# Split products in two column halves, and two PSUM banks that take turns at every inner tile

## The chip, the cores and the metric

The kernel runs on one core of one Trainium2 chip. The metric is the device time of one execution in microseconds (us), the median of several runs of the same program.

## The reference, cut to what matters

The reference is two transformer-like blocks over 512 tokens of width 1024, in float32. The first has a modulated norm, one wide input projection, a gated convolution branch, a four-head mLSTM and a feed-forward of width 2816. The second has two layers: sparse latent attention and windowed attention, each with a small cross-attention to a memory and a feed-forward with a three-tap convolution. What the change touches is the dense products, all of this kind:

```
proj = jnp.einsum("bsd,de->bse", h, w_in[l]) + b_in[l]
gt, up = jnp.split(jnp.einsum("bsd,df->bsf", h, w_ffn_up[l]), 2, axis=-1)
x = x + g2 * jnp.einsum("bsf,fd->bsd", jax.nn.silu(gt) * up, w_ffn_down[l])
```

The feed-forward products occur three times, once for each block or layer.

## The kernel before

Activations lie transposed: 128 channels on the partitions, 512 tokens in the free dimension, one such tile for every 128 channels. A product therefore has a 128x128 weight tile as the stationary operand of TensorE and a 128x512 activation tile as the moving one, and it fills one PSUM bank (512 float32 values per partition).

To be exact enough at the speed of the fp32r type, each operand is split in a high and a low part (`h_hi`, `h_lo`; for weights the two parts of `w_split`). Each inner tile `c` is then three fp32r matmuls into the same bank: weights high with activations high, weights high with activations low, weights low with activations high. The program gives one instruction for each; the trace shows a weight load (PEld) and a matmul (PE) for it. Plain float32 matmuls, used for small things such as rotations and means, leave two pairs of records each.

The work is a fixed list of jobs (`STAGES`, with names such as `glu`, `ffn0_up0`, `ffn0_down0`). An ordinary job is a weight block of 8 inner tiles and 2 output tiles: 48 matmuls, 24 into each of the two banks `2p` and `2p+1`, where `p` is the parity of the job. The two parities are double buffers of weights and of banks. A feed-forward down job has one output tile and 12 or 10 inner tiles. SyncE loads the weights, ScalarE writes their high part, GpSimd subtracts to get the low part, and VectorE and ScalarE take the banks over. TensorE's order is written out by hand:

- `split_job` (L901) issues nearly all the jobs. Where `waits` is given, in the first job of a stage whose activations come tile by tile, its order is inner tile outside and output tile inside, so the two banks already take turns at every inner tile. Without `waits` it does all inner tiles of the first bank and then those of the second. `product_done[p]` is raised once, after the job's last matmul. `between` is a list of small pieces of other work, of which one is taken after each tile with an odd index `m * kc + c`.
- `first_part` and `second_part` (L1040, L1059) issue the first two `glu` jobs, `tile_product` (L1137) the `o` and `merge_mlstm` tiles, `heads_part` (L1358) output jobs that fill in attention, and L1445, L1471, L1485 and L1533 the jobs `a_qmem`, `a_uk`, `a_uv` and `b_qmem`.
- The jobs `v` (L1111) and `b_v` (L1520) are not touched. In them the roles are turned: an activation tile of 128x128 is stationary, and a weight tile of 128x256 is the moving operand, in the same three fp32r matmuls. Each has a weight load of its own, also where two in a row have the same stationary tile.
- `rotations` (L1288) are float32 matmuls on 512 columns that come through `between`, above all in `a_keys`, `a_kv`, `b_v` and `b_qmem`; VectorE takes their banks over.

Of the kernel before, what the change touches and what calls it, by code (L numbers as in the profile page):

```python
# [31 lines left out]
P = 128  # L32
T = 512
TB = T // P
D = 1024
DT = D // P
# [181 lines left out]
def build(nc, io):  # L218
    ctx = ExitStack()
    with ctx:  # L220
# [624 lines left out]
        def _(pe):  # L845
# [36 lines left out]
            def late_mean(norm):  # L882
# [4 lines left out]
                    nc.tensor.matmul(banks[6][:], con("mean_d"), square[:, 1, :], start=True, stop=True)  # L887
                nc.tensor.matmul(banks[4][:], con("mean_d"), rstd[:], start=True, stop=True).then_inc(S["late_mean"], 1)

            def split_job(p, kc, width, rhs, waits, tiles=2, split=None, between=(), late=None):  # L890


                between = list(between)
                w = [(split or w_split)[p][:, part, 0:kc * width].rearrange("p (c n) -> p c n", n=width) for part in range(2)]

                order = [(m, c) for c in range(kc) for m in range(tiles)] if waits else [(m, c) for m in range(tiles) for c in range(kc)]
                for m, c in order:
                    if waits and m == 0:
                        pe.wait_ge(S[waits[0]], waits[1] + c + 1)
                    for wp, hp in ((0, 0), (0, 1), (1, 0)):  # L900
                        last = nc.tensor.matmul(banks[2 * p + m][:], w[wp][:, c, m * P:(m + 1) * P], rhs(c, hp),  # L901
                                                start=(c == 0 and wp + hp == 0), stop=(c == kc - 1 and wp == 1))
                    if between and (m * kc + c) % 2 == 1:
                        between.pop(0)()
                    if late and (m, c) == (1, 5):
                        late_mean(late)
                assert not between
                last.then_inc(product_done[p], 1)
# [121 lines left out]
            def first_part(c, m):  # L1030

                if (c, m) == (0, 0):
                    pe.wait_ge(S["half_lower"], 1)
                    pe.wait_ge(bank_free[p], use + 1)
                if (c, m) == (DT // 2, 0):
                    pe.wait_ge(lo_ready[p], SPLITS_BEFORE[FIRST["glu"]] + 1)
                if m == 0:
                    pe.wait_ge(S["norm_ready"], c + 1)
                for wp, hp in ((0, 0), (0, 1), (1, 0)):
                    last = nc.tensor.matmul(banks[2 * p + m][:], w[wp][:, c, m * P:(m + 1) * P], h_parts(c, hp),  # L1040
                                            start=(c == 0 and wp + hp == 0), stop=(c == DT - 1 and wp == 1))
                if (c, m) == (DT - 1, 1):
                    last.then_inc(product_done[p], 1)

# [3 lines left out]
            def second_part(c):  # L1048

                if c == 0:  # L1050
                    pe.wait_ge(bank_free[p2], use2 + 1)
                    pe.wait_ge(S["half_lower"], 2)
                if c == DT // 2:
                    pe.wait_ge(lo_ready[p2], SPLITS_BEFORE[FIRST["glu"] + 1] + 1)
                for m in (1, 0):
                    if (c, m) == (0, 0):
                        pe.wait_ge(S["norm_scaled"], DT)
                    for wp, hp in ((0, 0), (0, 1), (1, 0)):
                        last = nc.tensor.matmul(banks[2 * p2 + m][:], w2[wp][:, c, m * P:(m + 1) * P], h_parts(c, hp),  # L1059
                                                start=(c == 0 and wp + hp == 0), stop=(c == DT - 1 and wp == 1))  # L1060
                if c == DT - 1:
                    last.then_inc(product_done[p2], 1)

# [62 lines left out]
            def tile_product(k, between=None):  # L1126

                name, j, m = ("o", "merge_mlstm")[k // 8], k % 8 // 2, k % 2
                p, use = one(name, j)
                if m == 0:  # L1130
                    pe.wait_ge(lo_ready[p], SPLITS_BEFORE[FIRST[name] + j] + 1)
                if k >= 2:
                    pe.wait_ge(S["tile_free"], k - 1)
                w = [w_split[p][:, part, :].rearrange("p (c n) -> p c n", n=2 * P) for part in range(2)]
                for c in range(DT):
                    for wp, hp in ((0, 0), (0, 1), (1, 0)):
                        last = nc.tensor.matmul(banks[m][:], w[wp][:, c, m * P:(m + 1) * P], h_parts(c, hp),  # L1137
                                                start=(c == 0 and wp + hp == 0), stop=(c == DT - 1 and wp == 1))
                    if between and c == between[0]:
                        between[1]()  # L1140
                last.then_inc(product_done[p] if m else S["tile_done"], 1)
# [206 lines left out]
            def heads_part(name, j, k):  # L1348

                p, use = one(name, j)  # L1350
                before = GROUPS_BEFORE[k] // TB
                pe.wait_ge(lo_ready[p], SPLITS_BEFORE[FIRST[name] + j] + 1)
                pe.wait_ge(bank_free[p], use + 1)
                w = [w_split_out[p][:, part, :].rearrange("p (c n) -> p c n", n=P) for part in range(2)]
                for c in range(OUT_K):
                    pe.wait_ge(S["at_low"], before + (DT if c < DT else OUT_K))
                    for wp, hp in ((0, 0), (0, 1), (1, 0)):
                        last = nc.tensor.matmul(banks[2 * p][:], w[wp][:, c, :], out_split[name][hp][:, c, :] if c < DT else mem_split[hp][:, c - DT, :],  # L1358
                                                start=(c == 0 and wp + hp == 0), stop=(c == OUT_K - 1 and wp == 1))
                    if c == OUT_K - 1:  # L1360
                        last.then_inc(product_done[p], 1)
                    yield c
# [79 lines left out]
            for i in range(2 * DT * 3):  # L1442
                m, c = divmod(i // 3, DT)
                wp, hp = ((0, 0), (0, 1), (1, 0))[i % 3]
                last = nc.tensor.matmul(banks[2 * p + m][:], w[wp][:, c, m * P:(m + 1) * P], h_parts(c, hp),  # L1445
                                        start=(c == 0 and wp + hp == 0), stop=(c == DT - 1 and wp == 1))
                if i == 2 * DT * 3 - 1:
                    last.then_inc(product_done[p], 1)
                latent(i)
                if i in DOTS_AFTER:  # L1450
                    next(dot)
# [12 lines left out]
            for hd in range(A_HEADS):  # L1464
                if hd == 2:
                    pe.wait_ge(*emptied("a_q", 3))
                if hd >= 4:
                    pe.wait_ge(S["k_taken"], hd - 3)
                for c in range(2):
                    for wp, hp in ((0, 0), (0, 1), (1, 0)):  # L1470
                        last = nc.tensor.matmul(k_bank(hd)[:], uk[wp][:, c, hd * P:(hd + 1) * P], kv_split[hp][:, c, :],  # L1471
                                                start=(c == 0 and wp + hp == 0), stop=(c == 1 and wp == 1))
                last.then_inc(S["k_made"] if hd < A_HEADS - 1 else product_done[p], 1)
                if hd == 3:
                    rotate_queries(3)
            p = start_split("a_uv", 0)
            for n in range(2 * TB):
                b, half = divmod(n, 2)
                if n < 2:
                    pe.wait_ge(S["rot_sin_ready"], 15 + n)  # L1480
                else:
                    pe.wait_ge(S["v_taken"], n - 1)
                for c in range(2):
                    for hp, wp in ((0, 0), (0, 1), (1, 0)):
                        last = nc.tensor.matmul(banks[6 + n % 2][:], kv_split[hp][:, c, b * P:(b + 1) * P],  # L1485
                                                uv[wp][:, c, half * T:(half + 1) * T], start=(c == 0 and wp + hp == 0), stop=(c == 1 and hp == 1))
                last.then_inc(S["v_made"] if n < 2 * TB - 1 else product_done[p], 1)
            pe.wait_ge(S["rope_ready"], 18)
            pe.wait_ge(S["pool_tiles"], DT + TB - 1 + A_HEADS)
# [40 lines left out]
            def mem_queries(k):  # L1530
                m, c = divmod(k, DT)
                for wp, hp in ((0, 0), (0, 1), (1, 0)):
                    last = nc.tensor.matmul(banks[2 * p + m][:], mem_part[wp][:, c, m * P:(m + 1) * P], h_parts(c, hp),  # L1533
                                            start=(c == 0 and wp + hp == 0), stop=(c == DT - 1 and wp == 1))
                if k == 2 * DT - 1:
                    last.then_inc(product_done[p], 1)

# [1424 lines left out]
```

## Time and profile before

| | |
|---|---|
| time, median of 3 runs | 2217.3 us (2217.08 to 2217.7) |
| profiled execution: span | 2216.7 us |
| TensorE matmul busy | 2197.2 us (99%), 10682 records |
| weight loads busy | 1734.1 us (78%), 10682 records |
| VectorE, ScalarE, GpSimd busy | 995.1, 887.9, 878.6 us (45%, 40%, 40%) |
| granted TensorE clock | full, except in the last of the 40 slices or so (mean 0.999) |

The result of a profiled execution holds its span only, from the first to the last instruction; it stands 0.6 us under the median of the runs. A matmul record lasts from the start of its columns to a modelled end, so records overlap: a stream of 512-column fp32r matmuls has records of about 394 ns that start every 230 ns or so. What a matmul costs in a stream is therefore read from start to start.

### The profile page before, as it was taken

Reading aid. Unit: us, or ns where it says so; the run is one execution under the profiler, and the core shown is the slowest. Engines: PE = TensorE matmul, PEld = TensorE weight load, DVE = VectorE, ACT = ScalarE, POOL = GpSimd, SP = SyncE. Lnnn points to the kernel's source line nnn. Section 1 sums busy time; section 2 is a strip of 40 time slices with the busy share of each in tenths; the row PEclk is TensorE's granted clock in tenths of the full one; section 3 lists DMA queues with packets and bytes.
Section 4 is the critical chain, followed back from the end, with each engine's and each line's share of the span. In section 5 each row is a group of like instructions: output and inputs, shape, how many; then the busy total and the mean of one; then the engine's idle time right before and its main releaser. Section 6 shows DMA issues by size and latency. Waiting matters only on the chain.

```text
span 2216.7 us, 28735 instructions
## 1 busy us (share of the span) xinstructions
PE 2197.2 (99%) x10682; PEld 1734.1 (78%) x10682; DVE 995.1 (45%) x1904; ACT 887.9 (40%) x1301; POOL 878.6 (40%) x293
## 2 busy tenths in 40 slices
PE   9999999999999999999999999999999999999998
PEld 6888977788888888775777888888786678888886
DVE  4779687473311011358984333033205933330332
ACT  3345445452432123415375443233423944422332
POOL 3443422533344444453813443443434034444433
PEclk9999999999999999999999999999999999999999
DMA  9653321225232332331202432332420034323322
GB/s 365 224 170 115 96 77 58 85 92 171 66 98 78 109 98 73 108 86 38 77 1 72 114 95 83 107 95 73 153 78 24 2 91 114 95 81 108 95 70 82
DMA packets 302200, 216.89 MB, mean 98 GB/s; under 512 B 12960, under 2 KB 287520, under 8 KB 299680
## 3 DMA queue, kind: packets, MB, share of 16 engines
q1 hardware_dynamic: 293216, 195.80, 29.6%
q10 hardware_dynamic: 8896, 19.92, 2.6%
q8 instruction: 54, 0.88, 0.2%
q14 instruction: 34, 0.28, 0.0%
HBM read 213.61 MB, written 2.10 MB: 97 GB/s over the span
## 4 chain that ended last, share of the span: by engine, by line
PE 92%; DVE 2%; issue 2%; ACT 2%; DMA 1%; POOL 1%; SPq 0%; DVEq 0%; ACTq 0%; POOLq 0%
PE bank L901 72%; PE bank L1137 4%; PE bank L1111 2%; PE bank L1332 1%; PE bank L1310 1%; PE bank L1259 1%; DMA wslots<-in_w_glu 1%; PE bank L1319 1%; PE bank L1420 1%; PE bank L1159 1%; PE bank L1288 1%; PE bank L1358 1%; PE bank L1445 1%; DVE bank L2194 1%; PE bank L1170 1%
## 5 line engine op out<-in xcount | busy, mean ns | idle before, releaser
L2719 POOL TENSOR_TENSOR w_split<-wslots,w_split 128x2048 fp32r<-128x2048 f32 (+3 forms) x177 | 732.8, 4142 | 1039.5 <-ACT w_split L1598 520.7
L901 PE MATMUL bank<-h_hi,w_split 128*128 128x512 f32 x3312 | 1043.8, 394 | 0.0
L901 PEld LDWEIGHTS bank<-h_hi,w_split 128*128 128x128 f32 x3312 | 622.3, 188 | 140.6 <-issue 7.2
L901 PE MATMUL bank<-h_lo,w_split 128*128 128x512 f32 x1656 | 646.2, 390 | 0.0
L901 PEld LDWEIGHTS bank<-h_lo,w_split 128*128 128x128 f32 x1656 | 311.0, 188 | 72.7 <-issue 3.1
L1619 ACT ACTIVATE w_split<-wslots 128x2048 fp32r<-128x2048 f32 (+2 forms) x86 | 153.4, 1783 | 461.4 <-PE bank L901 461.4
L901 PE MATMUL bank<-hid_hi,w_split 128*128 128x512 f32 x1056 | 335.0, 397 | 1.0 <-DVE hid_lo L2476 1.0
L1598 ACT ACTIVATE w_split<-wslots 128x2048 fp32r<-128x2048 f32 (+3 forms) x85 | 147.7, 1737 | 335.1 <-PE bank L901 310.8
L901 PEld LDWEIGHTS bank<-hid_hi,w_split 128*128 128x128 f32 x1056 | 198.3, 188 | 49.3 <-DVE hid_lo L2476 1.9
L901 PE MATMUL bank<-hid_lo,w_split 128*128 128x512 f32 x528 | 207.5, 393 | 0.0
L2194 DVE SCALAR_TENSOR_TENSOR bank<-arena,cols,bank 128x512 f32<-128x512 f32 x240 | 161.4, 750 | 5.8 <-ACT bank L1712 5.2
L2474 DVE TENSOR_TENSOR bank<-arena,bank 128x512 f32<-128x512 f32 x66 | 46.0, 696 | 224.4 <-ACT arena L1932 224.4
L2719 POOL TENSOR_TENSOR w_split_out<-wslots,w_split_out 128x320 fp32r<-128x320 f32 (+1 forms) x28 | 49.5, 1786 | 190.9 <-ACT w_split_out L1598 190.9
L901 PEld LDWEIGHTS bank<-hid_lo,w_split 128*128 128x128 f32 x528 | 99.0, 188 | 24.5
L2609 DVE TENSOR_TENSOR bank<-bank,rstd 128x512 f32<-128x512 f32 x44 | 30.8, 700 | 165.9 <-PE bank L901 165.5
L2433 DVE TENSOR_TENSOR xT<-xT,bank 128x512 f32 (+1 forms) x24 | 16.5, 688 | 153.2 <-PE bank L901 153.2
L1137 PE MATMUL bank<-h_hi,w_split 128*128 128x512 f32 x256 | 84.3, 399 | 0.0
L2476 DVE TENSOR_TENSOR hid_lo<-bank,hid_hi 128x512 f32 x66 | 45.7, 692 | 57.2 <-ACT hid_hi L1934 57.2
L2009 ACT ACTIVATE arena<-arena,small 128x257 f32<-128x257 f32 (+5 forms) x128 | 64.2, 503 | 17.4 <-DVE small L2551 10.5
L1934 ACT ACTIVATE hid_hi<-bank 128x512 f32 (+1 forms) x66 | 39.6, 600 | 55.6 <-DVE bank L2474 55.6
L560 DVE TENSOR_TENSOR bank<-bank,xT 128x512 f32<-128x512 f32 x24 | 16.8, 700 | 95.9 <-PE bank L901 81.3
L2614 DVE SCALAR_TENSOR_TENSOR arena<-bank,cols,arena 128x511 f32<-128x511 f32 x44 | 33.0, 750 | 58.9 <-ACT arena L1928 58.9
(369 smaller groups left out, 2713.4 us busy)
## 6 DMA issues: line engine op xcount, KB each, us to landing
wslots<-in_f_w_up SPq DMA_DIRECT2D x88, 512.0 KB, 4.8
wslots<-in_w_in SPq DMA_DIRECT2D x24, 1024.0 KB, 5.4
wslots<-in_w_ffn_up SPq DMA_DIRECT2D x44, 512.0 KB, 4.5
arena<-in_w_ada ACTq DMA_DIRECT2D x8, 2048.0 KB, 8.9
wslots<-in_f_w_down SPq DMA_DIRECT2D x16, 768.0 KB, 4.8
wslots<-in_a_w_in SPq DMA_DIRECT2D x10, 1024.0 KB, 5.4
wslots<-in_f_w_down SPq DMA_DIRECT2D x16, 640.0 KB, 4.4
arena<-in_w_ada_first SPq DMA_DIRECT2D x8, 1024.0 KB, 20.5
```

The costliest lines, as they stand in the source:

```text
L901: last = nc.tensor.matmul(banks[2 * p + m][:], w[wp][:, c, m * P:(m + 1) * P], rhs(c, hp), start=(c == 0 and wp + hp == 0), stop=(c == kc ...
L1111: last = nc.tensor.matmul(banks[2 * p + b // 2][:, (b % 2) * 2 * P:(b % 2 + 1) * 2 * P], h_split[hp][:, c, b * P:(b + 1) * P], w[wp][:, c, :],
L1137: last = nc.tensor.matmul(banks[m][:], w[wp][:, c, m * P:(m + 1) * P], h_parts(c, hp), start=(c == 0 and wp + hp == 0), stop=(c == DT - 1 ...
L1598: nc.scalar.activation(split_of(JOB_STAGE[n], p)[:, 0, 0:size], slot(p, 1, size)[:, 0, :], ACT.Copy).then_inc(hi_ready[p], 1)
L1619: nc.scalar.activation(split_of(name, p)[:, 0, 0:size], slot(p, 1, size)[:, 0, :], ACT.Copy).then_inc(hi_ready[p], 1)
L1934: nc.scalar.activation(hid[0][:, 0:tiles, :][:, 2 * i + u, :], banks[2 * p][:], ACT.Copy).then_inc(S["hid_hi_ready"], 1)
L2009: last = nc.scalar.activation(part, part, ACT.Exp, bias=stat(n, 2 * with_sink + e), scale=-1.0, accum_out=stat(n, 4 + e))
L2194: ins = nc.vector.scalar_tensor_tensor(out=acc, in0=a_pad[:, c, k:k + T], scalar=dw_w[:, c, k:k + 1], in1=acc, op0=ALU.mult, op1=ALU.add)
L2474: nc.vector.tensor_tensor(banks[2 * p][:], up_gate[:, p, :], banks[2 * p + 1][:], ALU.mult).then_inc(S["hid_made"], 1)
L2476: nc.vector.tensor_tensor(hid[1][:, 0:tiles, :][:, t, :], banks[2 * p][:], hid[0][:, 0:tiles, :][:, t, :].bitcast(F32), ALU.subtract).then ...
L2614: steps.did(nc.vector.scalar_tensor_tensor(out=acc[:, 1:], in0=gates[:, 0:T - 1], scalar=w3[:, t, 1:2], in1=acc[:, 1:], op0=ALU.mult, op1= ...
L2719: last = nc.gpsimd.tensor_tensor(part[:, 1, cols_of], slot(p, 1, size)[:, 0, cols_of], part[:, 0, cols_of].bitcast(F32), ALU.subtract)
```

## The change

A helper issues each product as two matmuls, columns 0 to 255 and 256 to 511 of the same bank, with the same stationary tile. Only the first half of the first matmul of a bank has the start flag, only the second half of the last one the stop flag. All the products of the places named above go through it. And `split_job` uses the order with the inner tile outside in every job.

```diff
+            def by_halves(bank, w, x, start, stop):
+
+                for lo, hi in ((0, T // 2), (T // 2, T)):
+                    last = nc.tensor.matmul(bank[:, lo:hi], w, x[:, lo:hi], start=start and lo == 0, stop=stop and hi == T)
+                return last
+
             def split_job(p, kc, width, rhs, waits, tiles=2, split=None, between=(), late=None):
...
-                order = [(m, c) for c in range(kc) for m in range(tiles)] if waits else [(m, c) for m in range(tiles) for c in range(kc)]
+                order = [(m, c) for c in range(kc) for m in range(tiles)]
                 for m, c in order:
                     if waits and m == 0:
                         pe.wait_ge(S[waits[0]], waits[1] + c + 1)
                     for wp, hp in ((0, 0), (0, 1), (1, 0)):
-                        last = nc.tensor.matmul(banks[2 * p + m][:], w[wp][:, c, m * P:(m + 1) * P], rhs(c, hp),
-                                                start=(c == 0 and wp + hp == 0), stop=(c == kc - 1 and wp == 1))
+                        last = by_halves(banks[2 * p + m], w[wp][:, c, m * P:(m + 1) * P], rhs(c, hp),
+                                         c == 0 and wp + hp == 0, c == kc - 1 and wp == 1)
                     if between and (m * kc + c) % 2 == 1:
                         between.pop(0)()
...
```

The same replacement, matmul by `by_halves` with the same flags, is made at L1040, L1059, L1137, L1358, L1445, L1471, L1485 and L1533.

## Rows read from the trace of the kernel before

**Rows 1.** The page: its head, the engines' totals, the granted clock by slice, the chain.
```profile
span 2216.7 us, 28735 instructions
PE 2197.2 (99%) x10682; PEld 1734.1 (78%) x10682; DVE 995.1 (45%) x1904; ACT 887.9 (40%) x1301; POOL 878.6 (40%) x293
PEclk9999999999999999999999999999999999999999
PE 92%; DVE 2%; issue 2%; ACT 2%; DMA 1%; POOL 1%; SPq 0%; DVEq 0%; ACTq 0%; POOLq 0%
```
**Rows 2.** Whole span, for L901, L1137, L1358 and L1445: stretch, busy (x records), clock, DMA.
```profile
0.00:2217.00 2217.00, 1650.46 (x7104) 1332.14 (x7104) 1.00 0.32 98
0.00:2217.00 2217.00, 92.97 (x384) 70.78 (x384) 1.00 0.32 98
0.00:2217.00 2217.00, 30.49 (x120) 21.74 (x120) 1.00 0.32 98
0.00:2217.00 2217.00, 18.19 (x48) 8.29 (x48) 1.00 0.32 98
```
**Rows 3.** Groups of L901, high parts of activations: count, then busy us and mean ns.
```profile
L901 PE MATMUL bank<-h_hi,w_split 128*128 128x512 f32 x3312 | 1043.8, 394 | 0.0
L901 PE MATMUL bank<-hid_hi,w_split 128*128 128x512 f32 x1056 | 335.0, 397 | 1.0 <-DVE hid_lo L2476 1.0
```
**Rows 4.** Timeline in ffn0_up0: start us, duration, engine; first and last of 23 such rows.
```profile
599.68 0.39 PE L901 MATMUL bank<-h_lo,w_split 128*128 128x512 f32 x1
...
614.79 0.39 PE L901 MATMUL bank<-h_lo,w_split 128*128 128x512 f32 x1
```
**Rows 5.** Timeline in a feed-forward down stage: first and last of 21 such rows.
```profile
1400.60 0.39 PE L901 MATMUL bank<-hid_lo,w_split 128*128 128x512 f32 x1
...
1414.60 0.39 PE L901 MATMUL bank<-hid_lo,w_split 128*128 128x512 f32 x1
```
**Rows 6.** Timeline in v, 256 columns: first and last of 25 such rows.
```profile
239.75 0.28 PE L1111 MATMUL bank<-w_split,h_lo 128*128 128x256 f32 x1
...
247.91 0.28 PE L1111 MATMUL bank<-w_split,h_lo 128*128 128x256 f32 x1
```
**Rows 7.** Timeline in v: a weight load and its matmul.
```profile
239.98 0.19 PEld L1111 LDWEIGHTS bank<-w_split,h_lo 128*128 128x128 f32 x1
240.09 0.28 PE L1111 MATMUL bank<-w_split,h_lo 128*128 128x256 f32 x1
```
**Rows 8.** L1111 as a source: weight loads and matmuls of v.
```profile
L1111 PEld LDWEIGHTS bank<-w_split,h_hi x256: 186/188/192, 222.1 to 267.3; 128*128 128x128 f32 x128
L1111 PE MATMUL bank<-w_split,h_hi x256: 276/276/384, 222.1 to 267.4; 128*128 128x256 f32 x128
```
**Rows 9.** Timeline in b_v, between two rotations (L1288).
```profile
1679.44 1.02 PE L1288 MATMUL bank<-arena,cons 128*128 128x512 f32 x2
...
1680.54 0.28 PE L1520 MATMUL bank<-w_split,h_lo 128*128 128x256 f32 x1
...
1681.60 0.28 PE L1520 MATMUL bank<-w_split,h_lo 128*128 128x256 f32 x1
1681.71 1.02 PE L1288 MATMUL bank<-arena,cons 128*128 128x512 f32 x2
```
**Rows 10.** Timeline in a_keys, two rotations with six 512-column products between them.
```profile
979.90 1.02 PE L1288 MATMUL bank<-arena,cons 80*80 80x512 f32 x2
...
982.15 1.02 PE L1288 MATMUL bank<-arena,cons 80*80 80x512 f32 x2
```
**Rows 11.** Timeline in ffn0_up0's first job, where the banks already take turns: first, last.
```profile
568.10 0.39 PE L901 MATMUL bank<-h_lo,w_split 128*128 128x512 f32 x1
...
571.53 0.39 PE L901 MATMUL bank<-h_lo,w_split 128*128 128x512 f32 x1
```
**Rows 12.** Chain in order of time: start us, us, what; a run of float32 records.
```profile
1602.84 13.81 PE bank L1259 x64
```
**Rows 13.** DMA queue that carries instructions: packets, MB, share of 16 engines.
```profile
q8 instruction: 54, 0.88, 0.2%
```

More of the change, by code:

```diff
@@ L1039, in first_part @@
                 for wp, hp in ((0, 0), (0, 1), (1, 0)):
-                    last = nc.tensor.matmul(banks[2 * p + m][:], w[wp][:, c, m * P:(m + 1) * P], h_parts(c, hp),
-                                            start=(c == 0 and wp + hp == 0), stop=(c == DT - 1 and wp == 1))
+                    last = by_halves(banks[2 * p + m], w[wp][:, c, m * P:(m + 1) * P], h_parts(c, hp),
+                                     c == 0 and wp + hp == 0, c == DT - 1 and wp == 1)
                 if (c, m) == (DT - 1, 1):
@@ L1058, in second_part @@
                     for wp, hp in ((0, 0), (0, 1), (1, 0)):
-                        last = nc.tensor.matmul(banks[2 * p2 + m][:], w2[wp][:, c, m * P:(m + 1) * P], h_parts(c, hp),
-                                                start=(c == 0 and wp + hp == 0), stop=(c == DT - 1 and wp == 1))
+                        last = by_halves(banks[2 * p2 + m], w2[wp][:, c, m * P:(m + 1) * P], h_parts(c, hp),
+                                         c == 0 and wp + hp == 0, c == DT - 1 and wp == 1)
                 if c == DT - 1:
@@ L1136, in tile_product @@
                     for wp, hp in ((0, 0), (0, 1), (1, 0)):
-                        last = nc.tensor.matmul(banks[m][:], w[wp][:, c, m * P:(m + 1) * P], h_parts(c, hp),
-                                                start=(c == 0 and wp + hp == 0), stop=(c == DT - 1 and wp == 1))
+                        last = by_halves(banks[m], w[wp][:, c, m * P:(m + 1) * P], h_parts(c, hp),
+                                         c == 0 and wp + hp == 0, c == DT - 1 and wp == 1)
                     if between and c == between[0]:
@@ L1357, in heads_part @@
                     for wp, hp in ((0, 0), (0, 1), (1, 0)):
-                        last = nc.tensor.matmul(banks[2 * p][:], w[wp][:, c, :], out_split[name][hp][:, c, :] if c < DT else mem_split[hp][:, c - DT, :],
-                                                start=(c == 0 and wp + hp == 0), stop=(c == OUT_K - 1 and wp == 1))
+                        last = by_halves(banks[2 * p], w[wp][:, c, :], out_split[name][hp][:, c, :] if c < DT else mem_split[hp][:, c - DT, :],
+                                         c == 0 and wp + hp == 0, c == OUT_K - 1 and wp == 1)
                     if c == OUT_K - 1:
@@ L1444, in _ @@
                 wp, hp = ((0, 0), (0, 1), (1, 0))[i % 3]
-                last = nc.tensor.matmul(banks[2 * p + m][:], w[wp][:, c, m * P:(m + 1) * P], h_parts(c, hp),
-                                        start=(c == 0 and wp + hp == 0), stop=(c == DT - 1 and wp == 1))
+                last = by_halves(banks[2 * p + m], w[wp][:, c, m * P:(m + 1) * P], h_parts(c, hp),
+                                 c == 0 and wp + hp == 0, c == DT - 1 and wp == 1)
                 if i == 2 * DT * 3 - 1:
@@ L1470, in _ @@
                     for wp, hp in ((0, 0), (0, 1), (1, 0)):
-                        last = nc.tensor.matmul(k_bank(hd)[:], uk[wp][:, c, hd * P:(hd + 1) * P], kv_split[hp][:, c, :],
-                                                start=(c == 0 and wp + hp == 0), stop=(c == 1 and wp == 1))
+                        last = by_halves(k_bank(hd), uk[wp][:, c, hd * P:(hd + 1) * P], kv_split[hp][:, c, :],
+                                         c == 0 and wp + hp == 0, c == 1 and wp == 1)
                 last.then_inc(S["k_made"] if hd < A_HEADS - 1 else product_done[p], 1)
@@ L1484, in _ @@
                     for hp, wp in ((0, 0), (0, 1), (1, 0)):
-                        last = nc.tensor.matmul(banks[6 + n % 2][:], kv_split[hp][:, c, b * P:(b + 1) * P],
-                                                uv[wp][:, c, half * T:(half + 1) * T], start=(c == 0 and wp + hp == 0), stop=(c == 1 and hp == 1))
+                        last = by_halves(banks[6 + n % 2], kv_split[hp][:, c, b * P:(b + 1) * P],
+                                         uv[wp][:, c, half * T:(half + 1) * T], c == 0 and wp + hp == 0, c == 1 and hp == 1)
                 last.then_inc(S["v_made"] if n < 2 * TB - 1 else product_done[p], 1)
@@ L1532, in mem_queries @@
                 for wp, hp in ((0, 0), (0, 1), (1, 0)):
-                    last = nc.tensor.matmul(banks[2 * p + m][:], mem_part[wp][:, c, m * P:(m + 1) * P], h_parts(c, hp),
-                                            start=(c == 0 and wp + hp == 0), stop=(c == DT - 1 and wp == 1))
+                    last = by_halves(banks[2 * p + m], mem_part[wp][:, c, m * P:(m + 1) * P], h_parts(c, hp),
+                                     c == 0 and wp + hp == 0, c == DT - 1 and wp == 1)
                 if k == 2 * DT - 1:
```

## The prediction

> **What bounds the kernel now.** I read the page's totals first: TensorE has a matmul in flight for 2197.2 of 2216.7 us at the full granted clock, and the chain that ended last is 92% TensorE [rows 1]. No other engine passes 45%. So the time is the number of TensorE instructions times their spacing, and next comes how many the change touches. L901 issues 7104 of the 512-column products, L1137 384 and L1358 120; L1040, L1059, L1445, L1471, L1485 and L1533 have 48 each, which is 288 [rows 2]. That is 7896 of 10682 records. Of L901's, 3312 read `h_hi` and 1056 `hid_hi` [rows 3]; the low parts are in one product of three, so 4968 read `h` and 1584 `hid`.
>
> Then the spacing, start to start, from the timeline. A repeat of three products has one with the low part, so two such rows with 22 repeats between them span 66 products. In an up stage 614.79 - 599.68 = 15.11 us, 228.9 ns each [rows 4]. In a down stage 14.00 us for 60 products, 233.3 ns [rows 5]. 512 columns at the full clock of 2.4 GHz are 213.3 ns, so each product pays 15.6 or 20 ns over its columns. This excess, over 7896 products some 130 us, is the only stock from which this change can draw, and the only one that it can enlarge.
>
> **The change part by part.** *Halves.* 7896 instructions become 15792, each of 256 columns with a weight load. The question is what such an instruction costs in a stream. The trace before has fp32r matmuls of 256 columns in `v`: 24 repeats, 72 instructions, in 247.91 - 239.75 = 8.16 us, 113.3 ns each [rows 6]. Two of them are 226.7 ns, under both spacings of the whole product. Their operands have turned roles (activations stationary, weights moving), so this is the nearest row and not the same thing.
>
> Steady streams at that rate give: 4968 products on `h`, less the 96 of `a_keys` and `a_kv` (interrupted, below), 4872 x (228.9 - 226.7 = 2.3 ns unrounded) = 11.1 us; 1584 on `hid` x 6.7 ns = 10.6 us; the other 1344, less 96 in `a_qmem` and `b_qmem`, 1248 x 2.3 = 2.8 us, if they run at the up stage's pace now. Sum 24.5 us less.
>
> *Interrupted streams.* In `b_v` rotations cut the stream in pieces of twelve 256-column matmuls. From one rotation to the next is 1681.71 - 1679.44 = 2.27 us [rows 9]. In `a_keys` a rotation and six 512-column products, the same columns, take 982.15 - 979.90 = 2.25 us [rows 10]. Halves gain nothing there, or lose 0.02 us in six products. I take nothing for the 192 products of those four jobs.
>
> The bounds of the halves' cost. From above in the gain: if the second half, having the same stationary tile, did without a load, it would cost little over its columns. Against it: in `v` the first two of every three matmuls share their tile, and yet there are 256 loads for 256 matmuls with `h_hi` [rows 8], so I leave it to a small chance. From the other side: inside a piece of `b_v` nine instructions take 1681.60 - 1680.54 = 1.06 us, 117.8 ns each [rows 9], 235.6 ns for two. That is the same form as in `v`, 4% slower. So one form has two paces, and which of them a stream falls in I can't derive. I take 113.3 since the touched jobs are mostly long unbroken streams, as `v` is and `b_v` is not; both ends stay in the range.
>
> *Bank turns.* The order with the inner tile outside exists already in every first job with `waits`. In `ffn0_up0`'s first job 571.53 - 568.10 = 3.43 us for 15 products, 228.7 ns [rows 11], against 228.9 in the later jobs, which fill one bank at a time. So turns cost and give nothing on TensorE. Behind it nothing moves either: `product_done` is raised once, at the job's end, so VectorE and ScalarE get both banks when they did before. What shifts is `between`: with two output tiles its pieces are taken after tiles 3 and 4, 7 and 8, and so on, no longer after every second one. A rotation can then follow its neighbour after three products and the next after nine. VectorE must empty a rotation bank in time for the one four later. The mean distance stays, four banks span it, and I take 0; the worst is some tenths of a microsecond for each of about 20 rotations, under 5 us.
>
> *Instructions.* TensorE's program grows by 7896 instructions. Even if all 0.88 MB of the larger instruction queue were TensorE's, that is less than double of 0.2% of the DMA time [rows 13]. `v` kept 113.3 ns over 8 us while weights were loading. I take 0.
>
> The sum: 2216.7 - 24.5 = 2192.2 us of span; the runs' median stands 0.6 us over the span, so 2193 us. The likeliest case's own range is 2188 to 2202: its low end has the 1248 other products at the down stage's pace now (1248 x 4.4 = 5.5 us more), its upper end a third of the gain lost at job starts and in rotations.
>
> **The rivals.**
>
> *The disturbed pace everywhere (slower).* Place: every stream of halves. Mechanism: a weight load starts with the matmul before it; in `v` the load of an `h_lo` tile starts at 239.98 us, and its matmul at 240.09, 0.11 us later, though the load's record is 0.19 us long [rows 7]. At 512 columns a load has twice that time. With halves every load must be through in one half's time, and if it is late by a few ns each time, the pace is `b_v`'s. Price: (4968 + 1344) x (235.6 - 228.9 = 6.7) = +42 us and 1584 x 2.3 = +3.6 us: 2263 us. It decides where a half takes over 114.5 ns on `h`. For it: `b_v`; against it: `v`, which stays at 113.3 once there, and `a_keys` against `b_v`, nearly even.
> The Trainium skill ("TensorE: Matmul & The Clock Gate", LDWEIGHTS) puts a load at its columns divided by 1.2 GHz, an estimate of 107 ns for 128: as long as a half's 256 columns at 2.4 GHz. By that rule loads have no slack left in halves, which speaks for this rival; the 113.3 ns of `v` [rows 6] agree with a load that just fits.
>
> *A fixed cost for each instruction, the column pace unchanged (slower).* 64 float32 records of 256 columns take 13.81 us, 215.8 ns each [rows 12]; two passes of 256 columns are 213.3 ns, so 2.5 ns for each record are not columns. If the rest of the excess goes with the columns, as it would where reading the moving operand limits the pace, a product costs 228.9 + 2.5. Price 7896 x 2.5 = +20 us: 2237 us. Against it: by this two instructions of `v` could not be under 228.9, and they are.
> The Trainium skill (same page, "Back-to-back issue gap") has the same form, columns over 2.4 GHz plus 2.5 ns; by it each split costs 2.5 ns and nothing is gained.
>
> *Even.* Some streams fall in the one pace and some in the other; between -24.5 us with no product at 235.6 ns and +46 us with all, gain and loss meet at about a third (24.5 / 70); from three to four tenths the time is within 0.2% of before, 2213 to 2222 us.
>
> *The second half needs no load.* Half a product at 106.7 + 2.5 ns, twice, is 218.4: 6312 x 10.5 + 1584 x 14.9 = 90 us less, 2127 us.
>
> **How the numbers follow.** Likeliest case 0.45, no load 0.02, even 0.13, fixed cost 0.12, disturbed pace 0.28. What lies within 0.2% (4.4 us) can't be told from no change. So faster 0.47, same 0.13, slower 0.40. The predicted time is 2193 us. The range must reach over into the slower cases: 2187 to 2260 leaves out the case without loads, the outer tail of the likeliest and about half of the disturbed pace.
>
> **What would show it.** In the changed trace: L901's `h` halves in an up stage start every 113.3 ns (this forecast), 117.8 (disturbed) or 115.7 (fixed cost); the same on `hid`; the number of PEld records against PE records (equal, or the case without loads); `v` itself unchanged; the chain still over 90% TensorE and the clock full. The prediction is wrong if halves on `h` take over 114.5 ns, or if idle time of TensorE before rotations grows by more than 5 us.

## The result, and the profile after

The changed kernel takes 2256.5 us against 2217.2 us in the same session, ratio 1.0176 with a 95% interval of 1.0162 to 1.0191: slower, where 2193 us was forecast.

The page of the changed kernel, head, totals, clock, the chain's shares and the instruction queue, and then L893 (the matmul of `by_halves`) over the whole span:
```profile
span 2254.8 us, 44527 instructions
PE 2236.7 (99%) x18578; PEld 2118.4 (94%) x18578; DVE 995.6 (44%) x1904; ACT 887.6 (39%) x1301; POOL 876.5 (39%) x293
PEclk9999999999999999999999999999999999999999
PE 95%; issue 1%; ACT 1%; DVE 1%; POOL 1%; DMA 0%; DVEq 0%; SPq 0%; ACTq 0%; POOLq 0%
q8 instruction: 85, 1.39, 0.3%
0.00:2255.00 2255.00, 1894.83 (x15792) 1867.95 (x15792) 1.00 0.32 96
```
This shows that the 7896 products [rows 2] are 15792 matmuls with 15792 weight loads, that no load was saved, that the clock is full as before [rows 1], and that the chain is still TensorE. The cost is in the spacing, the time from one start to the next. Timeline of the changed kernel in the up stage of [rows 4] and the down stage of [rows 5], first and last of 21 rows each (a repeat, the three products of one inner tile, is now six halves), and in `v`, first and last of 25:
```profile
600.09 0.40 PE L893 MATMUL bank<-h_lo,w_split 128*128 128x256 f32 x2
...
614.22 0.40 PE L893 MATMUL bank<-h_lo,w_split 128*128 128x256 f32 x2
...
1400.29 0.40 PE L893 MATMUL bank<-hid_lo,w_split 128*128 128x256 f32 x2
...
1414.43 0.40 PE L893 MATMUL bank<-hid_lo,w_split 128*128 128x256 f32 x2
...
239.81 0.28 PE L1117 MATMUL bank<-w_split,h_lo 128*128 128x256 f32 x1
...
247.97 0.28 PE L1117 MATMUL bank<-w_split,h_lo 128*128 128x256 f32 x1
```
14.13 and 14.14 us for 120 halves are 117.8 ns each, in both stages, so 235.6 ns a product against 228.9 and 233.3. `v` is where it was, 8.16 us for 72, 113.3 ns. That is the disturbed pace, nearly everywhere. But not quite everywhere. Timeline of the changed kernel at the end of `b_q` and in the next job, `b_k`, with eight one-column float32 records between:
```profile
1685.62 0.40 PE L893 MATMUL bank<-h_lo,w_split 128*128 128x256 f32 x2
...
1689.86 0.40 PE L893 MATMUL bank<-h_lo,w_split 128*128 128x256 f32 x2
1690.10 0.39 PE L893 MATMUL bank<-h_hi,w_split 128*128 128x256 f32 x2
1690.42 1.05 PE L1505 MATMUL bank<-cons,rstd 1*128 1x1 f32 x8
...
1691.73 0.39 PE L893 MATMUL bank<-h_lo,w_split 128*128 128x256 f32 x2
...
1697.17 0.39 PE L893 MATMUL bank<-h_lo,w_split 128*128 128x256 f32 x2
```
Six repeats take 4.24 us before the interruption (117.8 ns a half) and eight take 5.44 us behind it (113.3 ns). The same line with the same tensors has both paces within 12 us. The experiments start from that.

### The profile page after: what moved, and what is told of

Same layout as the page of the kernel before. It is cut to its first block, busy times and chain, and to the rows that moved or that the text cites. A ratio compares the mean times of both kernels' runs of the same rounds, so it can differ in the third digit from the quotient of the medians.

```text
span 2254.8 us, 44527 instructions
## 1 busy us (share of the span) xinstructions
PE 2236.7 (99%) x18578; PEld 2118.4 (94%) x18578; DVE 995.6 (44%) x1904; ACT 887.6 (39%) x1301; POOL 876.5 (39%) x293
## 4 chain that ended last, share of the span: by engine, by line
PE 95%; issue 1%; ACT 1%; DVE 1%; POOL 1%; DMA 0%; DVEq 0%; SPq 0%; ACTq 0%; POOLq 0%
PE bank L893 81%; PE bank L1117 2%; PE bank L1338 1%; PE bank L1316 1%; PE bank L1265 1%; PE bank L1325 1%; PE bank L1426 1%; PE bank L1165 1%; PE bank L1294 1%; PE bank L1176 1%; PE bank L1526 0%; POOL w_split_out L2725 0%; PE bank L974 0%; PE bank L1005 0%; DMA xT<-in_x 0%
## 5 line engine op out<-in xcount | busy, mean ns | idle before, releaser
L893 PE MATMUL bank<-h_hi,w_split 128*128 128x256 f32 x7392 | 1198.8, 282 | 0.1
L893 PEld LDWEIGHTS bank<-h_hi,w_split 128*128 128x128 f32 x7392 | 1007.1, 188 | 29.2 <-issue 28.7
L893 PE MATMUL bank<-h_lo,w_split 128*128 128x256 f32 x3696 | 734.6, 280 | 0.0
L893 PEld LDWEIGHTS bank<-h_lo,w_split 128*128 128x128 f32 x3696 | 565.0, 188 | 4.6 <-issue 4.6
L893 PE MATMUL bank<-hid_hi,w_split 128*128 128x256 f32 x2112 | 336.2, 280 | 0.9 <-DVE hid_lo L2482 0.9
L893 PEld LDWEIGHTS bank<-hid_hi,w_split 128*128 128x128 f32 x2112 | 285.9, 188 | 1.3 <-DVE hid_lo L2482 1.3
L893 PE MATMUL bank<-hid_lo,w_split 128*128 128x256 f32 x1056 | 209.6, 279 | 0.0
L893 PEld LDWEIGHTS bank<-hid_lo,w_split 128*128 128x128 f32 x1056 | 161.6, 188 | 0.0
L1316 PE MATMUL bank<-arena 64*128 64x256 f32 (+5 forms) x256 | 54.4, 417 | 0.9 <-ACT arena L2113 0.7
```

What stands on the lines that cost most here:

```text
L893: last = nc.tensor.matmul(bank[:, lo:hi], w, x[:, lo:hi], start=start and lo == 0, stop=stop and hi == T)
L1316: last = nc.tensor.matmul(score_bank(g0 + g, e)[:, 0:n], q, kk, start=True, stop=True)
```

## The experiments

**Which edit costs it.** `e1_turns_only` has the new order alone, `e2_halves_only` the halves alone.

```diff
-                order = [(m, c) for c in range(kc) for m in range(tiles)] if waits else [(m, c) for m in range(tiles) for c in range(kc)]
+                order = [(m, c) for c in range(kc) for m in range(tiles)]      # e1: only this; e2: all but this
```


> Only the new order in split_job, whole products of 512 columns. Theory 'the halves cost it all': the time stays within 0.2% of before (2217 us) and the products on h start every 228.9 ns. Rival 'the bank turns cost': 10 us or more above before, and the spacing over 230 ns.

> Only the halves, in the order of before. Theory 'the halves cost it all': 2256 us, and a half starts every 117.8 ns, as with both edits. Rival 'the turns keep the halves from v's pace', since v writes 24 matmuls in a row into one bank: 113.3 ns and 2193 us.

Measured: e1 2217.4 us, ratio 1.0001 (0.9991 to 1.0010); e2 2256.9 us, ratio 1.0176 (1.0159 to 1.0193), with 12.01 us for 102 halves in `ffn0_up0`, 117.7 ns. The halves cost all of it and the turns nothing.

**What `v` has and the halves don't: output columns, order of parts, roles.** e3 puts the half outside the inner tiles, so that 24 matmuls in a row write the same columns; e11 takes `v`'s order of parts.

```diff
-                order = [(m, c) for c in range(kc) for m in range(tiles)]
+                runs = [(m, c, lo) for c in range(kc) for m in range(tiles) for lo in (0, T // 2)] if waits or between else [(m, c, lo) for m in range(tiles) for lo in (0, T // 2) for c in range(kc)]      # e3
...
-                    for wp, hp in ((0, 0), (0, 1), (1, 0)):
+                    for wp, hp in ((0, 0), (1, 0), (0, 1)):        # e11
```


> Halves, but in split_job's jobs without waits and without other work between, all inner tiles of columns 0 to 255 of a bank come before those of columns 256 to 511, so that 24 matmuls in a row write the same columns, each with another pair of tiles, as in v. Rival 'alternating columns (or the same stationary tile twice) cost 4.5 ns': 113.3 ns in ffn0_up0, about 2200 us. Theory 'a weight load for every 107 ns of columns sets 117.8, whatever the output columns': 117.8 ns and 2256 us.

> The changed kernel, but in split_job the three products of a tile come in v's order of parts: high with high, weights low with activations high, weights high with activations low. Theory 'the pace is history and phase': 117.8 ns in most streams, perhaps 113.3 in some. Rival 'the order of the parts makes v's pace': 113.3 ns everywhere in L893, 2193 us.

Measured: e3 2261.1 us, ratio 1.0196 (1.0176 to 1.0217), and 11.66 us for 99 halves, 117.8 ns; e11 2255.1 us (one run), 11.31 us for 96, 117.8 ns. Neither the output columns, nor that the same stationary tile comes twice in a row, nor the order of the parts makes `v`'s pace in a feed-forward. But both runs have the fast pace somewhere that the changed kernel has the slow one: e3 in `glu` (13.94 us for 123 halves from 58 us, 113.3 ns), e11 in `a_idx` (27.20 us for 240 from 962 us, 113.3 ns).

```diff
+                            for hp, wp in ((0, 0), (0, 1), (1, 0)):         # e7, jobs without waits
+                                last = nc.tensor.matmul(banks[2 * p + b // 2][:, (b % 2) * 2 * P:(b % 2 + 1) * 2 * P],
+                                                        rhs(c, hp)[:, b * P:(b + 1) * P], w[wp][:, c, :], ...
```


> In split_job's jobs with two output tiles of 8 inner tiles, no waits and nothing between, the operands change roles as in v: an activation tile of 128x128 is stationary, 256 columns of weights move. The same number of 256-column matmuls as in the changed kernel, but the banks then hold the product with tokens on the partitions, so the output is another. Theory 'which tensor is stationary and which moves decides between the two paces': 113.3 ns in ffn0_up0 and glu, and the time falls by about 4.5 ns x 8800 = 40 us to 2217 us. Rival 'v's pace comes from its start (a stall before it)': 117.8 ns stays in most jobs and the time stays near 2256 us.

Measured: 2246.2 us, ratio 1.0133 (1.0104 to 1.0163), between the two expectations. Timeline of e7 in `ffn0_up0`, where jobs with turned roles (L907) and jobs of halves (L893) alternate:
```profile
575.73 0.40 PE L893 MATMUL bank<-h_lo,w_split 128*128 128x256 f32 x2
...
578.56 0.40 PE L893 MATMUL bank<-h_lo,w_split 128*128 128x256 f32 x2
...
581.00 0.28 PE L907 MATMUL bank<-w_split,h_lo 128*128 128x256 f32 x1
...
584.74 0.28 PE L907 MATMUL bank<-w_split,h_lo 128*128 128x256 f32 x1
...
590.86 0.39 PE L893 MATMUL bank<-h_lo,w_split 128*128 128x256 f32 x2
...
594.94 0.39 PE L893 MATMUL bank<-h_lo,w_split 128*128 128x256 f32 x2
...
601.75 0.28 PE L907 MATMUL bank<-w_split,h_lo 128*128 128x256 f32 x1
...
605.99 0.28 PE L907 MATMUL bank<-w_split,h_lo 128*128 128x256 f32 x1
```
In order: halves 2.83 us for 24 (117.9 ns), turned 3.74 for 33 (113.3), halves 4.08 for 36 (113.3), turned 4.24 for 36 (117.8). Each kind of job has each pace, so roles don't decide. What happens between two jobs is regular: in this stage the pace goes over unchanged from a turned job to one of halves, all six times (the last into the down stage), and changes to the other one from halves to turned, all six times (at 579.7 us slow to fast, at 601.4 fast to slow, and so on). With the addresses of before, a stream has two paces, and which one it takes depends on what came before it. Inside a job it keeps the one it has, in all but one place of the traces of before, after, e2, e3, e7, e10, e11 and e20: early in `glu` (43.6 and 43.5 us) e3 and e10 go from slow to fast, with a single spacing of 120 ns between. They stay fast until 76 us, a stretch that the changed kernel does at the slow pace. That `v` is in the faster pace because of how it began would fit this, but no run shows it by itself.

**Does the weight load set it?** e4 cuts products in quarters of 128 columns. e8 and e9 halve the stationary tile, for halves and for whole products.

```diff
-                for lo, hi in ((0, T // 2), (T // 2, T)):
+                for lo, hi in ((0, P), (P, 2 * P), (2 * P, 3 * P), (3 * P, T)):     # e4
...
+                    n = P // 2 if w.shape[-1] == P and not start and not stop else P
+                    last = nc.tensor.matmul(bank[0:n, lo:hi], w[:, 0:n], x[:, lo:hi], ...   # e8; e9 with the one piece (0, T)
```


> Each product as four matmuls of 128 columns, everything else as in the changed kernel. Theory 'the weight load sets the pace of a half': a quarter takes as long as a half, 113 to 118 ns, a product 453 to 471 ns, and the time is near 4000 us. Rival 'columns set the pace and the load is hidden': a quarter takes 59 ns, and the time stays near 2256 us. Rival 'a fixed cost of a few ns per instruction over columns': 53.3 + 11.1 = 64.4 ns, 258 ns a product, about 2430 us.

> The changed kernel, but the stationary tile has 64 columns instead of 128 in all of its halves except those of a bank's first and last product: half the output channels get a wrong sum; the moving columns are the same. Theory 'the weight load sets a half's pace': with half the load the pace drops under 113 ns, to 107 to 110, and the time to 2150 to 2200 us. Rival 'reading the moving operand sets it': 117.8 ns and 2256 us as before.

> As the last, stationary tiles of 64 columns, but whole products of 512 columns (order of the changed kernel). Theory 'the 15.6 ns over a whole product's columns are the load disturbing the stream': they fall by about half, to 220 ns, and the time to some 2150 us. Rival 'they belong to the moving columns': 228.9 ns and 2217 us.

Measured: e4 4212.9 us (one run). Its timeline in `mix_out`, then the clock row of its page and two stretches of it (span, PE busy, PEld, DVE, ACT, POOL, clock, DMA):
```profile
1201.02 0.61 PE L893 MATMUL bank<-h_lo,w_split 128*128 128x128 f32 x4
1201.46 1.06 PE L893 MATMUL bank<-h_hi,w_split 128*128 128x128 f32 x8
1202.36 0.61 PE L893 MATMUL bank<-h_lo,w_split 128*128 128x128 f32 x4
...
PEclk9555559899999999999999999999998999999999
560.00:700.00 140.00, 140.00 (x853) 137.36 (x853) 51.53 (x89) 36.93 (x68) 30.47 (x8) 0.70 0.17 52
1195.00:1210.00 15.00, 15.00 (x102) 13.07 (x102) 2.69 (x4) 3.53 (x4) 1.21 (x1) 1.00 0.00 1
```
Twelve quarters take 1.34 us, 111.7 ns each, for 53.3 ns of columns. A quarter costs almost what a half costs, as the expectation had it for a pace set by the load. A quarter with a narrower stationary tile, which would tell the load from any other fixed time for each instruction, wasn't run. In five of the first six of the 40 slices the granted clock is at its lower level (1.2 GHz) for nearly all the time. TensorE issued such quarters and short pieces between, before it fell and while it was low; later the same quarters run at the full one. At the lower level a quarter takes (timeline of e4 at 600 us)
```profile
600.93 1.05 PE L893 MATMUL bank<-h_lo,w_split 128*128 128x128 f32 x4
601.79 1.91 PE L893 MATMUL bank<-h_hi,w_split 128*128 128x128 f32 x8
603.49 0.84 PE L893 MATMUL bank<-h_lo,w_split 128*128 128x128 f32 x3
```
2.56 us for twelve, 213 ns. So what paces a quarter, the load as I read it, needs twice the time at half the clock. The Trainium skill ("TensorE: Matmul & The Clock Gate", LDWEIGHTS) puts a load at its columns divided by 1.2 GHz and names no clock. By it 128 columns are an estimate of 107 ns: the 111.7 ns at the full clock is near that, the 213 ns at the half one is not.

For halves the length of the load is only a small part of the answer: e8 takes 2237.9 us (one run), with 11.91 us for 102 halves on `h`, 116.8 ns, and 11.80 for 102 on `hid`, 115.7. Half the load gives back 1.0 and 2.1 of the 11.1 ns over the columns; whether a load of any length costs the rest was not tested. e9 takes 2205.0 us (one run): 14.38 us for 63 whole products on `h`, 228.3 ns, and 13.75 for 60 on `hid`, 229.2, where 228.9 and 233.3 stood. So in up stages the length of the load adds next to nothing to a whole product, and in down stages 4 ns.

**Addresses.** Padding before the arena moves the split weights, `h_lo`, `hid` and all else in it, but not `h_hi`.

```diff
+        sb("pad", [P, 16])       # e5 (whole products), e6 (halves): 64 bytes; e12: [P, 64], 256 bytes
         arena = sb("arena", [P, ARENA])
```


> The changed kernel with 64 bytes of padding before the arena, so that the split weights start at a multiple of 1024 bytes of a partition instead of 64 bytes before one. Theory 'addresses decide between the two paces': the pace on h or hid leaves 117.8 ns for 113.3, in one direction or both, and the time moves by 5 us or more. Rival 'the roles or the load alone decide': 117.8 ns and 2256 us.

> The kernel before (whole products) with 64 bytes of padding before the arena. Theory 'addresses set how far the spacing stands over the columns': the spacing in an up stage moves by 1 ns or more from 228.9, or in a down stage from 233.3, and the time by some 5 to 15 us. Rival 'addresses matter for halves only': 228.9, 233.3 and 2217 us.

> The kernel before with 256 bytes of padding before the arena. Theory 'addresses matter, by their place within 256 bytes or less': the same spacings as without padding, 228.9 and 233.3, 2217 us. Rival 'by a larger unit': other spacings than without padding, up or down by 1 ns or more.

Measured: e6 2264.7 us, ratio 1.0217 (1.0187 to 1.0246), with 117.3 ns on `h` at 600 us and 118.9 at 800; e5 2233.8 us, ratio 1.0074 (1.0045 to 1.0103), 14.61 us for 63, 231.9 ns in the up stage; e12 2217.6 us, ratio 1.0001 (0.9989 to 1.0012), 228.9 ns. In e6 `v` lost its 113.3 ns for 117.9, though nothing of it was edited. Addresses count, and padding of 256 bytes leaves every spacing where it was. What counts is where operands start relative to each other: in e5's down stages `hid_hi`, `hid_lo` and `w_split` have all moved by the same 64 bytes, and a product still takes 233.3 ns (39.90 us for 171). By the shapes of the allocations, `h_hi`, `h_lo` and `hid_hi` start at one place within 256 bytes in the kernel before, and `w_split` and `hid_lo` 64 bytes short of it. The next three move these.

```diff
-        taken[0] = PROBS_AT
+        taken[0] = PROBS_AT + 16         # e14: hid_lo alone, 64 bytes
         hid.append(split_region("hid_lo", HALVES[0][1], T))
...
+        taken[0] += 16                   # e15, e16, e21; e18: 32. ARENA grows by as much
         w_split_at = taken[0]
```


> The kernel before (whole products), with hid_lo moved up by 64 bytes, so that hid_hi and hid_lo start at the same place within 256 bytes, as h_hi and h_lo do. Theory 'two moving tensors at different places within 256 bytes cost the down stages their 4.4 ns': 228.9 ns in the down stages, 1584 x 4.4 = 7 us less, 2210 us. Rival 'the width of the down jobs or their single bank costs it': 233.3 ns and 2217 us.

> The kernel before, with the split weights and all that lies behind them (hid_lo too) moved up by 64 bytes; h stays. Weights and activations then start at the same place within 256 bytes. Theory 'the place of the weights against the moving tensor sets the excess': up and down stages have one spacing, another than 228.9, up or down by 1 ns or more. Rival 'only the moving tensors' places against each other count': 228.9 in the up stages and, since hid_lo moves too, in the down stages.

> As the last, but moved by 128 bytes. Theory 'the place of the weights counts': another spacing in the up stages than 228.9. Rival 'only the moving tensors against each other': 228.9 in the up stages, and over it in the down stages, where hid_hi and hid_lo are 64 bytes apart again.

Measured: e14 2211.1 us, ratio 0.9971 (0.9959 to 0.9982), as the theory had it; e15 2198.3 us and e18 2242.2 us (one run each). Timelines of e14 in the down stage (23 rows), then e15 in the up stage (23) and e18 in the up stage (22):
```profile
1399.64 0.39 PE L901 MATMUL bank<-hid_lo,w_split 128*128 128x512 f32 x1
...
1414.75 0.39 PE L901 MATMUL bank<-hid_lo,w_split 128*128 128x512 f32 x1
```
```profile
599.71 0.39 PE L902 MATMUL bank<-h_lo,w_split 128*128 128x512 f32 x1
...
614.67 0.39 PE L902 MATMUL bank<-h_lo,w_split 128*128 128x512 f32 x1
```
```profile
599.77 0.39 PE L902 MATMUL bank<-h_lo,w_split 128*128 128x512 f32 x1
...
614.47 0.40 PE L902 MATMUL bank<-h_lo,w_split 128*128 128x512 f32 x1
```
15.11 us for 66 products is 228.9 ns where 233.3 stood [rows 5]; 14.96 for 66 is 226.7; 14.70 for 63 is 233.3. In e15 the down stage is at 226.7 too (13.60 us for 60), and in e18 at 234.6 (13.37 us for 57). The 226.7 ns that the forecast wanted from two halves is what a whole product takes once its operands' addresses agree within 256 bytes. Only steps of 64 bytes were tried, and which pair of operands costs what was not taken apart.

**Do halves gain from it too?**

> The changed kernel (halves and turns) with the split weights and what lies behind them moved up by 64 bytes, as in e15, where whole products fell to 226.7 ns. Theory 'the pairing of addresses sets the excess of halves as of whole products': 113.3 ns for a half on h, about 2200 us. Rival 'halves have a cost of their own, since each must wait for its load': 117.8 ns or more (v, with the same widths, went up to 120.7 ns in e15), 2256 to 2300 us.

Measured: 2292.7 us, ratio 1.0340 (1.0321 to 1.0359): the worst of all with halves. Timeline of e16 in `ffn0_up0`, 18 rows, the first beginning with the second half of its product, so 101 halves:
```profile
599.75 0.28 PE L894 MATMUL bank<-h_lo,w_split 128*128 128x256 f32 x1
...
611.87 0.40 PE L894 MATMUL bank<-h_lo,w_split 128*128 128x256 f32 x2
```
12.12 us, 120.0 ns. `v` in e15 has 120.0 ns as well (7.92 us for 66; the 120.7 of the expectation is a little too high). The best place for 512 columns is the worst tried for 256. Why is open.

**Can a stream be brought into the fast pace?** e10 puts a few other matmuls once into running streams, e20 one at every job's start in the feed-forwards.

```diff
+                    if (m, c) == (0, 0) and stage_now[0][:4] == "ffn0":
+                        nc.tensor.matmul(banks[2 * p][:, 0:1], con("mean_d"), cons[:, 0:1], start=True, stop=True)
...                                                  # e20, ffn1: fp32r, 32 columns; ffn2: fp32r, 384 columns
```


> The changed kernel with a few extra matmuls once before the second up stage of each feed-forward, in the middle of an unbroken stream of halves at 117.8 ns; their results are overwritten. Before ffn0_up1 three of v's form (roles turned, 256 columns), before ffn1_up1 one of 512 columns, before ffn2_up1 three of 384 columns. Theory 'two paces of the same instructions, kept from job to job, and a change in the stream flips it': after at least one of the three the halves on h run at 113.3 ns for the rest of the up stage (960 instructions or so, 4 us less). Rival 'halves on h and w_split in a stream of their own fall back': 117.8 ns within a few instructions after each, and 2257 us.

> The changed kernel with one extra matmul at the start of each job of the feed-forwards, overwritten later: ffn0 a float32 one of a single column, ffn1 an fp32r one of 32 columns, ffn2 an fp32r one of 384 columns. Theory 'a short stall at a job's start moves a stream to the fast pace': in at least one feed-forward most jobs run at 113.3 ns behind it. Rival 'the slow pace is the stable one for these operands': 117.8 ns in all three, and 2270 us with the extra matmuls' own time.

Measured: e10 2255.4 us, ratio 1.0171 (1.0142 to 1.0201). None of its three insertions did anything at its place: 117.8 ns behind each. Yet in `a_idx`, from 957 to 994 us, its stream is fast, in code that e10 didn't touch (15 repeats below, 10.20 us, 113.3 ns); in the changed kernel the same jobs run at 117.8. e11 was fast at this same place:
```profile
956.67 0.39 PE L893 MATMUL bank<-h_lo,w_split 128*128 128x256 f32 x2
...
966.87 0.39 PE L893 MATMUL bank<-h_lo,w_split 128*128 128x256 f32 x2
```
e20 takes 2268.8 us (one run) with its extra matmuls. Timeline of e20 in `ffn0_up0`, around one of the float32 columns:
```profile
603.13 0.39 PE L895 MATMUL bank<-h_lo,w_split 128*128 128x256 f32 x2
...
608.57 0.39 PE L895 MATMUL bank<-h_lo,w_split 128*128 128x256 f32 x2
608.79 0.39 PE L895 MATMUL bank<-h_hi,w_split 128*128 128x256 f32 x2
609.02 0.28 PE L909 MATMUL bank<-cons 128*128 128x1 f32 x2
609.16 0.48 PE L895 MATMUL bank<-h_hi,w_split 128*128 128x256 f32 x2
609.48 0.39 PE L895 MATMUL bank<-h_lo,w_split 128*128 128x256 f32 x2
```
5.44 us for 48 halves, 113.3 ns, and so in both up stages of `ffn0` in every job but the first. The insertion costs 0.23 us (0.91 instead of 0.68 for the repeat around it) and a job of 96 halves gains 0.43. In `ffn0`'s down stages and in `ffn1` and `ffn2` nothing changed, 117.8 ns. So on `h` the fast pace can be entered by one of the three kinds of disturbance. The column came again before every job, so e20 doesn't show how long one insertion would hold it. What exactly the entry needs stays open. The time of the run is no measure of the idea: the insertions of `ffn1` and `ffn2` cost time and gained none.

**The version that beats both**, e15's kernel in five runs:

> The kernel of e15 again, whole products with the split weights moved up by 64 bytes. From its spacing, 226.7 ns against 228.9 and 233.3, the time is 2198 us within 2 us, ratio to before 0.991; the rival is that the one run was lucky, and the ratio is over 0.995.

Measured: 2198.4 us, ratio 0.9915 (0.9901 to 0.9928) to the kernel before.

## Why the prediction was wrong

The measured 2256.5 us lies inside the stated range, near the end that was opened for the rival of the disturbed pace; the forecast itself went the wrong way, and its own sign of being wrong, over 114.5 ns for a half on `h`, came true.

*What bounds it, and the stock.* Right. All of the time moved by the spacing of TensorE's instructions, and no other engine came near the path: the chain is 95% TensorE.

*"I take 113.3 since the touched jobs are mostly long unbroken streams, as `v` is and `b_v` is not."* This is the step that failed. The length of a stream doesn't choose its pace: the long streams of the feed-forwards stay at 117.8 ns to their end, and a job of 96 halves after an interruption has 113.3. The trace before could have told. Timeline of the kernel before in two neighbouring pieces of `b_v`, each between two rotations, first and last low part of each:
```profile
1676.03 0.28 PE L1520 MATMUL bank<-w_split,h_lo 128*128 128x256 f32 x1
...
1677.05 0.28 PE L1520 MATMUL bank<-w_split,h_lo 128*128 128x256 f32 x1
...
1678.26 0.28 PE L1520 MATMUL bank<-w_split,h_lo 128*128 128x256 f32 x1
...
1679.32 0.28 PE L1520 MATMUL bank<-w_split,h_lo 128*128 128x256 f32 x1
```
Nine instructions take 1.02 us in the first, 113.3 ns each, and 1.06 us in the second, 117.8 ns. So pieces of the same short length, interrupted in the same way, have either pace, and the 117.8 ns [rows 9] is not the mark of an interrupted stream. The forecast picked one of two paces for 7896 products without a row that chose between them; what chooses is still open.

*Addresses.* No step and no rival had them, though the trace before held the question: 228.9 and 233.3 ns for the same shape in two stages [rows 4, 5] differ in the tensors read and in the form of the jobs (one output tile in the down stage). I took that difference as stock to be gained by halves (10.6 us on `hid`). e14, which moves `hid_lo` alone, shows it was `hid_lo`'s place; halves have 117.8 ns on both.

*The rival "disturbed pace everywhere".* It named the right place and pace. Its price was 46 us and the span grew by 38.1. The term most mis-sized is the other 1344 products, taken as if they stood at 228.9. If each product of before is set against its two halves, start to next start, the 1344 others cost 4.1 us more where the price had 9.0, L901's 4968 on `h` 30.6 (priced 33.3) and the 1584 on `hid` 3.5 (3.6), in all 38.2 us. The output jobs in the chain before took 50.26 us for 216 products, 232.7 ns, so there the way up to 235.6 was short. Its mechanism, a load a few ns late, is not confirmed: half the load gives back 1.0 ns of a half on `h` (e8).

*The fixed cost of 2.5 ns, and no load for the second half.* Both out: spacing 117.8 and not 115.7, and 15792 loads for 15792 matmuls.

*Bank turns.* Right, 0: e1's ratio is 1.0001. One thing was told wrong: `waits` goes to every job with `u == 0`, every second one of such a stage, not only the first, so before the change half of those jobs took turns already.

*Interrupted streams.* Right in size: in `a_keys` two neighbouring stretches between rotations, with twelve products, take 4.54 us in the changed kernel and took 4.50. The 2.25 and 2.27 us [rows 9, 10] were a hint I read too narrowly: the one direct comparison of 256 with 512 columns in the trace came out against the halves. As `b_v` has both paces, it could not have settled the matter either.

## What to carry to other kernels

A rate read from one stream is the rate of that stream, with its addresses and its start; where the same form shows a second rate elsewhere in the trace, both are candidates for the whole, and the forecast is worth no more than the reason to choose. Where fp32r matmuls of one shape have different spacings in different stages, compare where their operands start within 256 bytes before changing their shape: here 64 bytes of placement gave 0.85%, and splitting instructions cost 1.8%.

## What the runs showed of the hardware that I had not expected

- A 128x128x512 fp32r product takes 226.7, 228.9, 231.9, 233.3 or 234.6 ns in a stream, by where weights and activations start relative to each other within 256 bytes (e15, before, e5, e18, e18's down stages); padding of 256 bytes changes nothing (e12).
- 256-column fp32r matmuls have two lasting paces at one placement, 113.3 and 117.8 ns (the kernel before in `b_v`, e7, e10, e20), and 120.0 at another (e16). A job keeps its pace with rare exceptions; the next one can take it over or change it, regularly so in e7's `ffn0_up0`. Why is open: neither the length of the load (e8), the roles (e7), the output columns (e3) nor the order (e11) explains it.
- 128-column fp32r matmuls, each with a load of 128 columns, have a spacing of 111.7 ns at the full clock and 213 ns at the half one (e4), against 53.3 ns for their columns at the full clock. That the load sets it is my reading.
